# The last expert's down weights loaded into the gate weights' buffer, its fold placed inside the preceding down product, and one activation-table load for the final norm

## The reference, cut to what matters

```python
def expert_block(args):
    xb, e = args
    hb = jax.nn.silu(xb @ w_gate[e]) * (xb @ w_up[e])
    return hb @ w_down[e]
...
x = x + _hier_moe(hm, ...)        # the two expert outputs of a token, each times its weight
return _rms_norm(x, g_final)      # x * rsqrt(mean(x*x) + 1e-6) * g
```

## Time and profile before

| what | value |
|---|---|
| three timed runs | 2912.15, 2912.94 and 2915.98 us; median 2912.94 us |
| profiled execution | 2903.76 us, of which 2902.0 us are its span from first to last instruction |
| mean granted PE clock in it | 0.96 of full speed |
| busy | PE 92%, DVE 52%, POOL 39%, ACT 32% |

### The profile page before, as it was taken

The page is one execution under the profiler, slowest core; times in us unless marked ns, Lnnn a source line. Parts: engine busy times, 40 slices in busy tenths (PEclk is TensorE's granted clock), DMA queues, the critical chain, the costliest instruction groups (busy, mean ns, idle before and its releaser), DMA issues.

```text
span 2902.0 us, 37535 instructions
## 1 busy us (share of the span) xinstructions
PE 2671.0 (92%) x12686; PEld 2046.7 (71%) x12686; DVE 1515.1 (52%) x2147; ACT 930.1 (32%) x1525; POOL 1142.4 (39%) x768
## 2 busy tenths in 40 slices
PE   7989898999999888989999999999898699999994
PEld 4768777887867777777887877766676466666662
DVE  4684574212346764663213354133654678777784
ACT  4323332111013323321110021122302377776674
POOL 4651205666747741026666755332152011113110
PEclk9999999999999999999999999999999899999997
DMA  3212102332322112012333322211022299999995
GB/s 129 65 37 88 35 3 73 96 100 87 94 66 80 51 51 73 16 37 87 95 100 102 97 80 81 86 51 37 22 87 109 76 363 389 386 391 394 346 389 195
DMA packets 78151, 373.33 MB, mean 129 GB/s; under 512 B 11216, under 2 KB 11344, under 8 KB 53328
## 3 DMA queue, kind: packets, MB, share of 16 engines
q1 hardware_dynamic: 71888, 360.23, 35.4%
q0 software_dynamic: 5280, 8.40, 0.9%
q10 hardware_dynamic: 864, 3.15, 0.3%
HBM read 368.06 MB, written 12.58 MB: 131 GB/s over the span
## 4 chain that ended last, share of the span: by engine, by line
PE 80%; DVE 9%; issue 3%; POOL 3%; ACT 3%; DMA 1%; DVEq 0%; ACTq 0%; SPq 0%; POOLq 0%
PE PS L1930 16%; PE PS L1932 16%; PE PS L1931 16%; PE PS L2284 4%; PE PS L2406 4%; PE PS L2407 4%; PE PS L2436 4%; PE PS L2307 4%; PE PS L2044 2%; PE PS L2416 2%; PE PS L2243 2%; PE PS L2298 1%; PE PS L1996 1%; PE PS L2394 1%; POOL arena L629 1%
## 5 line engine op out<-in xcount | busy, mean ns | idle before, releaser
L605 POOL TENSOR_SCALAR whi<-ring 128x1024 fp32r<-128x1024 f32 x260 | 290.6, 1118 | 1147.8 <-PE PS L1932 929.0
L608 POOL TENSOR_TENSOR wlo<-ring,whi 128x1024 fp32r<-128x1024 f32 x260 | 655.3, 2520 | 21.7
L1931 PE MATMUL PS<-xl,whi 128*128 128x512 f32 x1376 | 540.5, 393 | 0.0
L1930 PE MATMUL PS<-xh,whi 128*128 128x512 f32 x1312 | 525.1, 400 | 14.9 <-POOL wlo L608 6.9
L1932 PE MATMUL PS<-xh,wlo 128*128 128x512 f32 x1312 | 514.0, 392 | 0.0
L1689 DVE TENSOR_TENSOR arena_r<-arena,arena_r 128x1024 fp32r<-128x1024 f32 x256 | 301.6, 1220 | 85.3 <-ACT arena_r L1033 84.4
L1931 PEld LDWEIGHTS PS<-xl,whi 128*128 128x128 f32 x1376 | 261.3, 190 | 52.7 <-issue 2.9
L1930 PEld LDWEIGHTS PS<-xh,whi 128*128 128x128 f32 x1312 | 248.2, 189 | 69.5 <-issue 10.6
L1932 PEld LDWEIGHTS PS<-xh,wlo 128*128 128x128 f32 x1312 | 247.9, 189 | 52.9
L1033 ACT ACTIVATE arena_r<-arena 128x1024 fp32r<-128x1024 f32 x256 | 256.0, 1050 | 85.2 <-DMA arena<-w_gate 84.9
L1930 PE MATMUL PS<-xs,whi 128*128 128x512 f32 x496 | 208.7, 421 | 25.6 <-DVE xs L1147 15.5
(11 more groups left out here) (410 smaller groups left out, 4556.9 us busy)
## 6 DMA issues: line engine op xcount, KB each, us to landing
ring<-ring_w SPq DMA_DIRECT2D x280, 512.0 KB, 3.5
arena<-w_gate SPq DMA_DIRECT2D x64, 1024.0 KB, 7.4
arena<-w_up SPq DMA_DIRECT2D x64, 1024.0 KB, 9.0
arena<-w_down SPq DMA_DIRECT2D x64, 1024.0 KB, 8.5
arena<-y_dram SPq DMA_DIRECT2D x8, 512.0 KB, 7.4
xT<-xT_in SPq DMA_DIRECT2D x1, 2048.0 KB, 8.5
out<-arena SPq DMA_DIRECT2D x4, 512.0 KB, 2.6
arena<-memT_in SPq DMA_DIRECT2D x1, 1024.0 KB, 7.5
```

The source lines that it names most:

```text
L605: nc.gpsimd.tensor_scalar(whi[:, t % 2, :], ring[:, t % RING, :], 1.0, 0.0, ALU.mult, ALU.add).then_inc(sems["whi"], 1)
L608: nc.gpsimd.tensor_tensor(wlo[:, t % RING, :], ring[:, t % RING, :], whi[:, t % 2, :], ALU.subtract).then_inc(sems["split"], 1)
L1930: mm(out, a[0], b[0], start=start, stop=False)
L1931: mm(out, a[0], b[1], start=False, stop=False)
```

## The change

It loads the last expert's down weights into the gate weights' buffer (`load_last`), each half as soon as PE has used that half of expert 31's gate weights. Their two split quarters go to the places of the gate weights' high and low parts. The fold of expert 31 (`turn_gu`) moves between the two halves of expert 30's down product, and its down product (`down_last`) follows, with quarters 2 and 3 first, into banks 2 and 3. `hT_last` is a place of its own for the hidden values. The last scatter copies its indices ahead of its wait for the result. In the final norm one table load stands ahead of the loop, and DVE scales tile qt-1 right after it has combined tile qt. The same is done in the branch that is not taken.

```diff
@@ -242,6 +242,7 @@
+        hT_last = at_(4096, 4, TB)
...
+
+        def last_of(i):
+            return 16 if i < NEXP // 2 else 32
...
+            def load_last(i, u, e):
+
+                for h in range(2):
+                    sp.wait_ge(MS["useG"], lin(i, u, 2, h + 1))
+                    lo = LOADED["G"] + 2048 * h
+                    sp.dma_start(arena[:, lo:lo + 2048], w_down[e][:, 2048 * h:2048 * h + 2048]
+                                 ).then_inc(MS["wL"][h], 16)
...
-            load("D", i, 1, NEXP - 1)
+            load_last(i, 1, NEXP - 1)
...
-            def scatter(i, u):
-
-                pool.wait_ge(MS["yea"], lin(i, u, 1, 1))
-                pool.wait_ge(MS["yev"], lin(i, u, 1, 1))
+            def scatter(i, u, last=False):
+
+                if last:
+                    pool.wait_ge(MS["yd"][u % 2], dma_of(i, u - 2))
+                else:
+                    pool.wait_ge(MS["yea"], lin(i, u, 1, 1))
+                    pool.wait_ge(MS["yev"], lin(i, u, 1, 1))
                 pool.sem_inc(MS["go"], 1)
                 nc.gpsimd.tensor_copy(idyi[0:TB, u % 2:u % 2 + 1], taby[:, i * 2 + u, :]).then_inc(MS["gy"], 1)
                 pool.wait_ge(MS["gy"], lin(i, u, 1, 1))
+                if last:
+                    pool.wait_ge(MS["yea"], lin(i, u, 1, 1))
+                    pool.wait_ge(MS["yev"], lin(i, u, 1, 1))
                 pool.sem_inc(MS["go"], 1)
                 pool.indirect_dma_start(y_dram.rearrange("k q p d -> (k q p) d"), bass.IndirectOffsetOnAxis(
                     ap=idyi[0:TB, u % 2:u % 2 + 1], axis=0), ysb[u % 2][0:TB, :], None, bounds_check=2 * T - 1, oob_is_err=False
@@ -686,12 +707,12 @@
                     scatter(i, u - 1)
 
...
-            scatter(NEXP // 2 - 1, 1)
+            scatter(NEXP // 2 - 1, 1, True)
...
-            def y_a(i, u):
+            def y_a(i, u, bank=5):
                 act_e.wait_ge(MS["useD"], lin(i, u, 2, 2))
                 act_e.wait_ge(MS["yd"][(u - 2) % 2], dma_of(i, u - 2))
-                nc.scalar.activation(ysb[u % 2][0:TB, 0:T], PS[0:TB, 5, :], ACT.Identity).then_inc(MS["yea"], 1)
+                nc.scalar.activation(ysb[u % 2][0:TB, 0:T], PS[0:TB, bank, :], ACT.Identity).then_inc(MS["yea"], 1)
 
             def moe_a(i, u, prev, next_):
...
                     highs("G", i, u + 1, range(2, 4))
+                else:
+                    last_a(i, u)
                 if prev:
                     y_a(i, u - 1)
 
-            def last_a(i):
-                silu(i, 1)
-                h_high(i, 1)
-                highs("D", i, 1, range(SPLIT_D))
-                y_a(i, 1)
+            def last_a(i, u):
+                act_e.wait_ge(MS["useG"], lin(i, u, 2, 2))
+                for k in range(SPLIT_D):
+                    act_e.wait_ge(MS["wL"][k // 2], last_of(i))
+                    nc.scalar.activation(high("G", k), loaded("G", k), ACT.Identity).then_inc(MS["highD"], 1)
+                silu(i, u)
+                h_high(i, u, hT_last)
 
             xgt_a(0, 0)
             blocks(act_e, moe_a, 0, NEXP)
-            last_a(NEXP // 2 - 1)
+            y_a(NEXP // 2 - 1, 1, 2)
...
+
+            tables["set"] = None
+            ln_exp_tables()
             for qt in range(QT):
                 act_e.wait_ge(MS["fa"], qt + 1)
...
+                else:
+                    last_v(i, u)
                 if prev:
                     y_v(i, u - 1)
 
-            def last_v(i):
-                hidden(i, 1)
-                h_low(i, 1)
-                lows("D", i, 1, range(SPLIT_D), SPLIT_D)
-                y_v(i, 1)
+            def last_v(i, u):
+                hidden(i, u, hT_last)
+                for k in range(SPLIT_D):
+                    v.wait_ge(MS["highD"], lin(i, u, SPLIT_D, k + 1))
+                    tt(low("G", k), loaded("G", k), high("G", k), ALU.subtract).then_inc(MS["lowD"], 1)
+                h_low(i, u, hT_last)
...
-            last_v(NEXP // 2 - 1)
+            y_v(NEXP // 2 - 1, 1, 3)
...
+            def scaled(qt):
+                v.wait_ge(MS["fs"], qt + 1)
+                nc.vector.scalar_tensor_tensor(out=yg[2 * qt], in0=yg[2 * qt], scalar=small[:, 8 + qt:9 + qt],
+                                               in1=gfin, op0=ALU.mult, op1=ALU.mult).then_inc(MS["ff"], 1)
...
-            for qt in range(QT):
-                v.wait_ge(MS["fs"], qt + 1)
-                nc.vector.scalar_tensor_tensor(out=yg[2 * qt], in0=yg[2 * qt], scalar=small[:, 8 + qt:9 + qt],
-                                               in1=gfin, op0=ALU.mult, op1=ALU.mult).then_inc(MS["ff"], 1)
+                if qt:
+                    scaled(qt - 1)
+            scaled(QT - 1)
...
-            def down(i, u):
+            def down(i, u, quarters=range(4)):
...
-                for k in range(4):
+                for k in quarters:
...
+            def down_last(i, u):
+                pe.wait_ge(MS["hm"], lin(i, u, 1, 1))
+                for k in (2, 3, 0, 1):
+                    pe.wait_ge(MS["wL"][k // 2], last_of(i))
+                    if k < SPLIT_D:
+                        pe.wait_ge(MS["hl"], lin(i, u, 1, 1))
+                        pe.wait_ge(MS["lowD"], lin(i, u, SPLIT_D, k + 1))
+                    for j in range(2):
+                        of = slice(T * j, T * j + T)
+                        out = PS[0:TB, 2 + j, :]
+                        if k < SPLIT_D:
+                            ins = mm3(out, [x[:, k, :] for x in hTs], (high("G", k)[:, of], low("G", k)[:, of]),
+                                      start=False, stop=(k == 1))
+                        else:
+                            ins = mm(out, hT_last[:, k, :], loaded("G", k)[:, of], start=(k == 2), stop=False)
+                    if k % 2:
+                        ins.then_inc(MS["useD"], 1)
...
-                if prev:
+                if prev and next_:
                     down(i, u - 1)
+                elif prev:
+                    down(i, u - 1, range(2))
+                    turn_gu(i, u)
+                    down(i, u - 1, range(2, 4))
+                    down_last(i, u)
 
             pe.wait_ge(MS["te"], 16)
             turn_x(0, 0)
             blocks(pe, moe_p, 0, NEXP)
-            turn_gu(NEXP // 2 - 1, 1)
-            down(NEXP // 2 - 1, 1)
```

More of the change, by code:

```diff
@@ L337, in build @@
         MS.update({k: [ctx.enter_context(nc.semaphore(f"m_{k}{u}")) for u in range(n)]
-                   for k, n in (("xg", 2), ("wG", 2), ("wU", 2), ("wD", 2), ("yd", 2), ("yg", QT))})
+                   for k, n in (("xg", 2), ("wG", 2), ("wU", 2), ("wD", 2), ("wL", 2), ("yd", 2), ("yg", QT))})
         def lin(i, u, mult=1, c=0):
@@ L574, in _ @@
             feed(i, 1, lambda d: NEXP - 1 + d, True, False)
-            load("D", i, 1, NEXP - 1)
+            load_last(i, 1, NEXP - 1)
             sp.wait_ge(MS["ro"], 1)
             with overflow(sp):
+                sp.wait_ge(MS["useD"], lin(i, 1, 2, 2))
+                sp.sem_inc(MS["wD"][0], 16)
+                sp.sem_inc(MS["wD"][1], 16)
                 ex = [sp.value_load(ovi[0:1, j:j + 1], min_val=0, max_val=NEXP - 1) for j in range(OVB)]
@@ L582, in _ @@
                     feed(i, j, lambda d: ex[j + d], False if j == 0 else "first" if j == 1 else True, j + 1 < OVB)
-                load("D", i, OVB - 1, ex[OVB - 1])
+                load_last(i, OVB - 1, ex[OVB - 1])
                 sp.wait_ge(MS["yd"][(OVB - 2) % 2], dma_of(i, OVB - 2))
@@ L693, in _ @@
                 blocks(pool, moe_g, NEXP, NEXP + OVB)
-                scatter((NEXP + OVB) // 2 - 1, 1)
+                scatter((NEXP + OVB) // 2 - 1, 1, True)
                 pool.wait_ge(MS["yd"][0], dma_of((NEXP + OVB) // 2 - 1, 0))
@@ L1069, in silu, with h_high @@
                 nc.scalar.activation(sT, PS[:, 4, 0:4 * TB], ACT.Silu).then_inc(MS["sl"], 1)
-            def h_high(i, u):
+            def h_high(i, u, h=hT):
                 act_e.wait_ge(MS["hm"], lin(i, u, 1, 1))
-                nc.scalar.activation(hTs[0][:, 0:SPLIT_D, :], hT[:, 0:SPLIT_D, :], ACT.Identity
+                nc.scalar.activation(hTs[0][:, 0:SPLIT_D, :], h[:, 0:SPLIT_D, :], ACT.Identity
                                      ).then_inc(MS["he"], 1)
-            def y_a(i, u):
+            def y_a(i, u, bank=5):
                 act_e.wait_ge(MS["useD"], lin(i, u, 2, 2))
                 act_e.wait_ge(MS["yd"][(u - 2) % 2], dma_of(i, u - 2))
-                nc.scalar.activation(ysb[u % 2][0:TB, 0:T], PS[0:TB, 5, :], ACT.Identity).then_inc(MS["yea"], 1)
+                nc.scalar.activation(ysb[u % 2][0:TB, 0:T], PS[0:TB, bank, :], ACT.Identity).then_inc(MS["yea"], 1)
             def moe_a(i, u, prev, next_):
@@ L1111, in _ @@
                 blocks(act_e, moe_a, NEXP, NEXP + OVB)
-                last_a((NEXP + OVB) // 2 - 1)
+                y_a((NEXP + OVB) // 2 - 1, 1, 2)
+            tables["set"] = None
+            ln_exp_tables()
             for qt in range(QT):
@@ L1863, in xgt_v, with hidden, h_low, y_v @@
```

(24 more changed lines are left out.)

## The result

| | before | changed |
|---|---|---|
| median of 20 timed runs each | 2916.34 us | 2897.52 us |
| ratio, 95% interval | | 0.994 (0.9919 to 0.9962) |
| the same in later rounds (29 and 12 runs) | 2902.47 us | 2898.92 us, 0.9979 (0.9949 to 1.001) |
| span of the profiled execution | 2902.0 us | 2894.9 us |

Single runs of one kernel lie some 35 us apart (2877.67 to 2910.59 for the changed one; two runs of the kernel before, 3408.61 and 9823.05, lie far outside of any spread). So I compare the traces from a fixed point: **time 0 is the start of expert 30's twelve split matmuls**, 2847.45 before and 2851.64 in the changed kernel. The two medians of the first line differ by 18.8 us; the end of the traces behind that point is 54.55 us before and 43.26 us now, 11.3 us shorter.

The account below looks back on a forecast made before the run. The prediction took PE, busy 92% of the span, as the bound, leaving the end to gain: 6.2 + 0.3 + 4.1 = 10.6 us, so 2912.94 - 10.6 = 2902.3 us, range 2896 to 2907.

Parts of the forecast that it names:

- the range of the sum alone: Whole kernel: bounds of the summed terms, 2901.2 to 2903.2 us, widened by three runs' spread to 2900.4 to 2906.2.
- its widening to 2896: Whole kernel: range lowered to 2896 us, by half the 9.2 us between profiled execution and median.
- Fold and down product: Last experts' end: reordered matmuls let the copies out of PSUM start 6.2 us earlier, bounds 5.8 to 6.3.
- That nothing waits: Last down product: moved loads, split and silu cost nothing, hidden under 1.73 + 3.58 us of other matmuls.
- Last scatter: Last scatter on POOL: copying its indices before the wait gains 0.3 us, or 1.06 if the issue time is overlapped.
- The 0.74 us of "issue": Last scatter: 0.74 us in the chain, taken as the DMA's own start, which stays.
- Norm: Final norm: one early table load makes DVE set the pace, gaining 4.1 us, bounds 3.6 to 4.3.
- The carried difference: Whole kernel: the profiled execution's 9.2 us under the timed median, unexplained, was carried over to the forecast median.
- the clock did not fall at the moved fold: Rival at expert 31's fold: lower clock from there costs 9.7 us, giving 2912, no change; chance 0.05.
- The transposes: Moved fold: a rule that PE-mode transposes do not count as busy PE was cited for the falling-clock rival.
- The load was not late: Rival at expert 31's first float32 matmul: PE waits for late weights, each us costing one, possibly 2924; chance 0.03.
- only behind an idle PE: Experts' end: the clock was said to fall only after PE idled, as argument against its falling at the fold.

Follow-up runs that it names:

- experiments 8 to 10: Changed kernel with DVE's scalings behind all combinations: norm 18.29 us; with new order but no table load: 23.78; with two scalings behind: 19.10; changed kernel itself: 19.18.
- Experiment 6: Changed kernel with the last down weights' loads also waiting for the first half of expert 30's down product; copies out of PSUM at 18.19 us, against 14.66.
- the filler: Changed kernel with two scalings behind, plus useless matmuls in the cross attention; timed ratio to before 0.9919 (0.9887 to 0.9952), median 2889.89 us.
- its filler: Kernel before with 14 useless matmuls behind expert 31's fold; copies out of PSUM at 18.61 us against 21.11, end 52.17 against 54.55.

## Why the prediction was right

The time, 2897.5, is in the range, and faster was the forecast; its 10.6 us (0.36%) lies just under the first interval (0.38% to 0.81%) and within the second. That the number landed is in part luck: the range of the sum alone, with the spread of three runs, was 2900.4 to 2906.2, and only its widening to 2896 reaches the median. The medians also differ by 18.8 us in the first rounds and by 3.6 in the later ones, where the traces show 11.3. What was right is the mechanism. Term by term, in the traces:

- *Fold and down product*, 6.2 forecast: 6.45. The new layout from one row of before was right to 0.25 us; the float32 group of expert 31 took 3.43, not 3.58. That nothing waits was right: halves landed 6.3 and 7.0 us behind their issue, hidden was ready 2.7 us ahead of PE's need, h_low 3.6.
- *Last scatter*, 0.3: 0.24. The 0.74 us of "issue" stayed when the index copy was long done, so they are no wait for it, as the term had assumed.
- *Norm*, 4.1: 4.57 to the last scaling's start. The term was 0.5 too small, since the handovers from the square to Ln and to Exp cost 0.02 to 0.04 us and not the tenths that I left for them, and the wait for the second tile was 0.23 shorter in this trace. What I did not see is that the order on DVE, which I took for harmless, gives 0.4 us of it back (experiments 8 to 10).
- *The carried difference.* I took the 9.2 us between the profiled execution and the median as a constant. It is none: executions differ by more than the whole effect, largely by two causes, of which one, the stall, stood in the trace of before (below). That the point forecast came out 4.8 us over the median is within that spread.

Of the rivals, the clock did not fall at the moved fold (windows, 1.00). The transposes that I set beside it are not what the fold is: `turn_gu` makes plain matmuls with a folding matrix, and only `turn_x` transposes. The load was not late. Experiment 6 fits that a us costs a us beyond the slack, at one point, but the path of that rival was wrong: I let the second half decide, while the first one holds up ACT's copies, silu and hidden, and had the smaller slack in my own working (2.0 against 3.2 us). My sentence that the clock fell "only behind an idle PE" holds in all traces of this end, but not the other way round: it fell behind gaps of 3.56 and 2.12 us and not behind one of 3.34. Why not there stays open.

## What to carry to other kernels

When a pipeline's last item stands by itself, look for a buffer that comes free an item earlier, and for work of the item ahead that can be cut in two to cover the handovers; buffer and order of the quarters together gave more here than the fold's place. In an epilogue with two engines, compare the work behind the last producer with the latency of what it waits for (1.2 against 1.75 us here), and test each half of an edit by itself: the table load gave all, and the new order took 0.4 us of it back. When single runs spread by more than the effect, measure from a fixed point near the change in the trace.

## What the runs showed that I had not expected

Two things ahead of time 0 carry much of the spread between the traces. They are not all of it: the first score of the cross attention starts between 2208.3 and 2220.3 us, so up to 12 us lie ahead of it, and I have not looked for their cause. In nine of the fourteen traces the cross attention falls to half the clock, in five it doesn't. Windows of the kernel before, then of the changed one, in the same stretch:

```profile
2212.00:2225.00 13.00, 11.63 (x66) 7.71 (x64) 7.36 (x20) 5.54 (x20) 3.39 (x2) 1.00 0.00 0
2225.00:2240.00 15.00, 12.81 (x74) 8.67 (x73) 8.86 (x25) 3.89 (x14) 0.00 (x0) 1.00 0.01 2
```

```profile
2212.00:2225.00 13.00, 11.63 (x44) 7.96 (x44) 5.45 (x14) 4.33 (x15) 3.38 (x2) 0.66 0.00 0
2225.00:2240.00 15.00, 14.91 (x49) 10.55 (x50) 6.12 (x15) 3.39 (x12) 0.00 (x0) 0.50 0.00 1
```

From its first score to the point where ACT takes up the sums of the next norm it takes 49.6 us at full clock (50.6 with the filler) and 63.8 to 65.3 at half, with the same instructions; in the pair of traces that I compared, it cost the changed kernel 14.2 us.

The other is a single stall among the experts. In six of the fourteen traces one scatter's row lasts 7.44 or 7.45 us in place of 0.93 (a few others 1.6 to 2.7), each time in the same part of the program (the row starts between 2644 and 2699 us), and never twice. From the first gather to time 0 those six took 543.4 to 552.8 us; of the eight others seven took 536.0 to 538.1 and one, with a row of 2.71, 542.7. In the kernel before the gather queued behind the stalled scatter on POOL came late, and PE waited for it:

```profile
2664.74 7.45 POOL L674 DMA_INDIRECT y_dram<-xT,idyi  x1 [0.88 <-POOL idyi L671]
2673.23 1.71 POOL L662 DMA_INDIRECT xT<-hm_dram,idxi  x1 [0.85 <-POOL idxi L659]
2681.99 1.97 PE L2394 MATMUL PS<-mats,xT 128*128 128x128 f32 x8 [5.12 <-DMA xT<-hm_dram,idxi]
```

The gap between two gate loads there is 26.1 us in place of 16.8. It struck the trace of before and not the first one of the changed kernel: from first gather to time 0 they took 545.76 and 536.05, so that 9.7 of the 14.2 us were taken back. The kernels with and without the change both show it, so it is not the change's. Without a stall the kernel before (with its filler, which stands behind time 0) took 536.49 us, and the changed kernel and its variants 536.02 to 538.06, so the change gains nothing ahead of time 0. Why a scatter's issue lasts so long in some executions, and why always equally long, stays open.
